# A two-layer encoder trunk: the recurrent scan without its engine loop, and squares for a norm taken in the gate before it

## The chip, the cores and the metric

The kernel runs on one core of a Trainium2 chip. The metric is the device time of one execution in microseconds (us), the median over runs. The engines are TensorE (PE in the rows), VectorE (DVE), ScalarE (ACT), GpSimd (POOL) and SyncE (SP); PEld is TensorE's weight load.

## The reference, cut to what matters

Two layers run over 1024 prompt and 64 sample positions of 1024 features. Layer 0 mixes tokens with a gated convolution and attention; layer 1 is a recurrent layer (RWKV-7). Each layer then has a channel mixer and a gated embedding:

```python
def rms_norm(x, g):
    y = x32 * lax.rsqrt(jnp.mean(x32 * x32, axis=-1, keepdims=True) + NORM_EPS)
    return (y * g.astype(jnp.float32)).astype(x.dtype)
...
        hn = rms_norm(h, W['mix_norm_pre'][i])
...
        gate = jax.nn.sigmoid(rms_norm(h, W['ple_norm'][i]) @ W['ple_gate'][i])
        h = h + gate * (p[i].astype(h.dtype) @ W['ple_proj'][i])
```

The recurrent mixer carries a state through time, per head of 64 (16 heads):

```python
    def step(S, inp):
        r_t, w_t, k_t, v_t, kk_t, b_t = inp
        sa = jnp.einsum('bhvk,bhk->bhv', S, -kk_t)
        S = S * w_t[:, :, None, :] + sa[..., None] * b_t[:, :, None, :] + v_t[..., None] * k_t[:, :, None, :]
        return S, jnp.einsum('bhvk,bhk->bhv', S, r_t)
```

## The kernel before, in words

All activations are feature-major: `H`, `A`, `B`, `TM` are SBUF tiles of 128 partitions by some 8, 8, 22 and 4 blocks of T = 1092 columns (both groups of positions with padding), `ps` is PSUM. Each engine has a hand-written program; they meet at semaphores. A class `Tally` counts what each semaphore will have reached. Inside `t.loop(n, ...)` a stretch is emitted once and repeated by the engine itself (`Fori`, L111, which sets a register, computes wait values from it and branches back), with the growth of each count per turn as arguments.

**The gated embedding** (`channel_mixer`, end). For each of the 8 blocks of features PE makes the gate's product (72 matmuls, L466) and the projection of `p` (6 matmuls, L440), ACT takes the sigmoid (L1270), DVE multiplies (L1848) and adds into `H` (L1851), and then splits the next weights into an upper and a lower part (L1578, L1579). DVE does it in `ple_tiles`: a loop of 3 turns of two blocks, and two blocks after it.

**The norm ahead of layer 1.** When the last block of `H` is there, ACT squares the 8 blocks one by one (L1071, called from the program's line L1284) into two alternating buffers of `TM`, and PE sums each over the features with a matrix of ones (`norm_direct`, L498, three matmuls per block, accumulated in PSUM). The two alternate, since a buffer is free again only when PE has read it. Then ACT takes the logarithm and the exponential (`root`, L1078 and L1081), and DVE scales the 8 blocks (`pre_norm`, L1537).

**The scan of layer 1** goes over 16 chunks of 64 prompt positions, then one of the sample. One chunk is one call of `chunk` on PE, ACT, DVE and POOL. Each pipelines three chunks: the state of chunk c (`from_state` L926 and L929, `solve` L937, `outputs` L952 and L955, `to_state` L962), the inverse of a triangular matrix for chunk c + 1 by five levels (`y` L903 on PE, copied by ACT L1424; `z` L912 on PE, taken by DVE L2040 and turned L2029), and the products of chunk c + 2 (`gram` L863, masked by DVE L2060 and L2066; `turn_n` L878). POOL loads chunk c + 3 and sets up a matrix (L2354). In each engine chunks 0 to 11 are a loop of three turns with four chunks in its body (PE's is at L1026 to L1029), and chunks 12 to 15 are written out behind it.

In the body of a loop a wait's value depends on the turn, so the queue computes it in a register ahead of the wait (L851 in `await_`); in written-out chunks it is a constant.

Of the kernel before, what the change touches and what calls it, by code (L numbers as in the profile page):

```python
# [24 lines left out]
ALU = mybir.AluOpType  # L25
# [5 lines left out]
KT = D // P  # L31
SEQ, DEC, PAST = 1024, 64, 2048
PAD = 2
P0 = PAD
S0 = PAD + SEQ + PAD
T = S0 + DEC
NCH = 3
CH = T // NCH
# [8 lines left out]
NP_ = PLE // P  # L47
HR = 16
NPAIR = HR // 2
C = 64  # L50
NCHUNK = SEQ // C
# [33 lines left out]
NL = len(LEVELS) - 1  # L85
# [54 lines left out]
def build_trunk(nc, I, O, stop=99):  # L140
    ctx = ExitStack()
    with ctx:
# [15 lines left out]
        H = sb("H", [P, KT, T])  # L158
# [70 lines left out]
        CV = [kv[:, PAST:2 * PAST].rearrange("p (b n) -> p b n", b=16) for kv in KV]  # L229
        Vt = Bf[:, 16 * T:16 * T + 9 * 512].rearrange("p (b n) -> p b n", b=9)  # L230
        HEAD = [slice(0, C), slice(C, P)]


        Lb = [{n: B[:, 4 * u + j, :] for j, n in enumerate("rkwa")} for u in range(2)]
# [53 lines left out]
        def k(name):  # L288
            o, n = CST[name]
            return cst[:, o:o + n]  # L290
# [7 lines left out]
        def pset(s):  # L298
# [12 lines left out]
        d_v = scratch("d_v", [NPAIR, P, (NCHUNK + 1) * C])  # L311


        names = ["setup", "held", "x_in", "mm_done", "read0", "read1", "w_used", "wl_ready", "xh_ready", "xl_ready", "h_out", "h_in", "sq_ready", "sq_used", "rs_ready",
                 "normed", "h_ready", "act_step", "dve_step", "pool_step", "out_done",
                 "wv_in", "wv_ready", "tm_free", "ax_ready", "p_in",
                 "cum_ready", "cum_out", "cum_in", "lf_e", "logf_out", "ckt_done", "ckt_ready", "mb_done", "mb_read", "x_add", "x_ready", "v_done", "r_log", "r_ready", "qn_ready", "cumk_in", "kv_in2", "kv_in3", "turn_done", "s_done", "s_read", "e_ready",
# [102 lines left out]
        def _(pe):  # L420
            t = Tally(pe)
# [332 lines left out]
                return  # L754


            norm_direct()
            t.up("normed", KT)
            X = [[B[:, 8 * b + j, :] for j in range(KT)] for b in range(2)]

# [262 lines left out]
                    gram(1, 1)  # L1023
                z(l, 1)
            turn_n(1, 0)
            with t.loop(3, z_dup=4, g_done=8, g_ready=8, tok_read=16, n_done=8, m_first=8, m_ready=8 * NL, n_ready=8, mt_ready=8 * NL,  # L1026
                        y_ready=8 * NL, c_in=8, a_ready=8, u_ready=8, oo_read=8):
                for c in range(4):
                    chunk(c)  # L1029
            for c in range(12, NCHUNK):  # L1030
                chunk(c, prepare=c + 2 <= NCHUNK)
            for g in range(2):
                await_("m_ready")
# [29 lines left out]
        def _(act):  # L1063
            t = Tally(act)

            def square(src, needs=None):

                j = t.n.get("sq_ready", 0) % 2
                if t.some("sq_ready", -1):
                    act.wait_ge(S["sq_used"], t.val("sq_ready", -1))  # L1070
                nc.scalar.activation(TM[:, j, :], src, ACT.Square).then_inc(S["sq_ready"], 1)  # L1071
                t.up("sq_ready")
# [206 lines left out]


            log_and_exp()
            act.wait_ge(S["h_ready"], t.val("h_ready"))
            for j in range(KT):
                square(H[:, j, :])  # L1284
            root()
            act.wait_ge(S["dve_p"], t.up("dve_p"))

# [197 lines left out]
                for g in range(2):  # L1485
                    take_y(g)
            turned_n(1, 0)
            with t.loop(3, y_done=8 * NL, n_done=8, tok_done=8, a_done=8, u_done=8, oo_done=8) as i:
                for c in range(4):
                    chunk(c, i * (4 * C) + (P0 + C * c))  # L1490
            for c in range(12, NCHUNK):
                chunk(c, P0 + C * c, prepare=c + 2 <= NCHUNK)
            for g in range(2):
                from_state(g)
# [33 lines left out]
        def _(dve):  # L1528
# [30 lines left out]
                dve.wait_ge(S["rs_ready"], t.up("rs_ready"))  # L1559

            def pre_norm(gain):
                t.up("sq_ready", KT)
                t.up("sq_used", KT)
                rstd()
                for j in range(KT):
                    stt(A[:, j, :], H[:, j, :], v1(gain, j), TM[:, 3, :], ALU.mult, ALU.mult).then_inc(S["normed"], 1)
                    t.up("normed")
# [212 lines left out]
            def channel_mixer(l):  # L1780
# [58 lines left out]
                def ple_tiles(i, last):  # L1839
                    for j in range(2):  # L1840
                        if not (last and j == 1):
                            split_chunk()
                            t.skip_chunks(1)
                        s, mm, rd = t.unit()
                        dve.wait_ge(S[f"read{s}"], rd)
                        s, mm, rd = t.unit()
                        dve.wait_ge(S["mm_done"], mm)
                        nc.vector.tensor_tensor(c3(TM[:, j, :]), pset(s), c3(TM[:, j, :]), ALU.mult).then_inc(S[f"read{s}"], 1)  # L1848
                        dve.wait_ge(S[f"read{s}"], rd)
                        h = H[:, KT - 2 + j, :] if last else H[:, bass.ds(i * 2 + j, 1), :].rearrange("p a n -> p (a n)")  # L1850
                        nc.vector.tensor_tensor(h, h, TM[:, j, :], ALU.add).then_inc(S["h_ready"], 1)  # L1851
                        t.up("h_ready")

                with t.loop(KT // 2 - 1, mm_done=4, read0=2, read1=2, h_ready=2, chunk=4, w0=16, w1=16, w2=16, w3=16,
                            wl_ready=2, wh=2, dve_step=2) as i:
                    ple_tiles(i, False)
                ple_tiles(None, True)

# [254 lines left out]
            for l in range(NL):  # L2113
# [7 lines left out]
                    masked(1, 1, 0)  # L2121
                    masked(1, 1, 1)
                take_z(0, l, 1)
            with t.loop(3, g_done=8, m_init=4, m_first=8, m_ready=8 * NL, z_done=8 * NL, st_done=8, st_read=8) as i:
                for c in range(4):
                    chunk(c, bass.ds(i * 4 + c, 1))
            for c in range(12, NCHUNK):
                chunk(c, slice(c, c + 1), prepare=c + 2 <= NCHUNK)
            for g in range(2):
                new_state(slice(NCHUNK, NCHUNK + 1), g)  # L2130
# [31 lines left out]
        def _(pool):  # L2162
# [214 lines left out]
            double_chunk(2)  # L2377
            pool.wait_ge(S["hs_out"], 16)
            pool.dma_start(H[:, :, :], d_h).then_inc(S["hs_in"], 16)
            with t.loop(3, u_done=8, tok_done=8, zi0=96, zi1=96) as i:  # L2380
                for c in range(4):
                    chunk(c, i * 4 + c)
            for c in range(12, NCHUNK):
                chunk(c, c, prepare=c + 2 <= NCHUNK, load=c + 3 <= NCHUNK)
            pool.wait_ge(S["c_in"], 2 + 2 * NCHUNK)
            store(O["wkv"][:, 0], ST)
# [148 lines left out]
```

## Time and profile before

| | us |
|---|---|
| median of 3 runs | 4018.39 |
| lowest, highest | 4010.32, 4018.71 |
| the profiled execution, its own time | 4018.97 |
| span of its trace | 4017.2 |
| mean granted clock of TensorE | 0.951 of full |

The page says for each engine how long it was busy (PE 91% of the span, DVE 38%, ACT 21%, POOL 5%), and in its part 4 which chain of work ended last. A wait is named by what released it; "issue" is time in which an engine waited for nothing that the profile shows. PEclk is the granted clock: 1.00 is 2.4 GHz, 0.50 is 1.2 GHz. The names of PEldq and the like are the queues that feed the engines.

### The profile page before, as it was taken

Reading aid. Unit: us, or ns where it says so; the run is one execution under the profiler, and the core shown is the slowest. Engines: PE = TensorE matmul, PEld = TensorE weight load, DVE = VectorE, ACT = ScalarE, POOL = GpSimd, SP = SyncE. Lnnn points to the kernel's source line nnn. Section 1 sums busy time; section 2 is a strip of 40 time slices with the busy share of each in tenths; the row PEclk is TensorE's granted clock in tenths of the full one; section 3 lists DMA queues with packets and bytes.
Section 4 is the critical chain, followed back from the end, with each engine's and each line's share of the span. In section 5 each row is a group of like instructions: output and inputs, shape, how many; then the busy total and the mean of one; then the engine's idle time right before and its main releaser. Section 6 shows DMA issues by size and latency. Waiting matters only on the chain.

```text
span 4017.2 us, 66019 instructions
## 1 busy us (share of the span) xinstructions
PE 3646.6 (91%) x28466; PEld 3290.3 (82%) x28466; DVE 1540.8 (38%) x2029; ACT 856.4 (21%) x1134; POOL 207.1 (5%) x347
## 2 busy tenths in 40 slices
PE   6999999899999999889988688888698999999977
PEld 4997337799999999666987577787488999999967
DVE  3143554432212222536338644444734221222352
ACT  2000332210000010228225323233422000001020
POOL 0000000000000000001002211110100000000000
PEclk8999998899999999899998799889999999999989
DMA  2122002111121130124226621111411112113111
GB/s 89 60 77 80 22 22 82 71 43 47 42 82 53 42 129 29 49 75 171 87 104 254 237 86 52 46 42 34 147 60 54 42 39 80 60 44 120 42 39 69
DMA packets 79399, 301.59 MB, mean 75 GB/s; under 512 B 13560, under 2 KB 15880, under 8 KB 75192
## 3 DMA queue, kind: packets, MB, share of 16 engines
q0 software_dynamic: 36816, 174.51, 11.9%
q1 hardware_dynamic: 42368, 123.92, 9.9%
q8 instruction: 172, 2.82, 0.3%
q14 instruction: 43, 0.35, 0.0%
HBM read 217.29 MB, written 81.10 MB: 74 GB/s over the span
## 4 chain that ended last, share of the span: by engine, by line
PE 73%; DVE 7%; issue 2%; ACT 2%; DMA 1%; POOL 0%; DVEq 0%; ACTq 0%; POOLq 0%
PE ps L466 55%; DVE A L1537 2%; PE ps L912 2%; PE ps L903 2%; PE ps L480 2%; PE ps L440 1%; PE ps L773 1%; PE ps L863 1%; DVE H L1618 1%; DVE A_r L1594 1%; PE ps L498 1%; PE ps L926 1%; PE ps L929 1%; PE ps L878 1%; DVE B L1537 1%
## 5 line engine op out<-in xcount | busy, mean ns | idle before, releaser
L466 PE MATMUL ps<-H_r,W_r 128*128 128x364 f32 (+1 forms) x3192 | 705.8, 329 | 0.0
L466 PE MATMUL ps<-H_r,TM_r 128*128 128x364 f32 x2736 | 607.5, 330 | 21.6 <-DVE A_r L1594 18.0
L466 PE MATMUL ps<-A_r,TM_r 128*128 128x364 f32 x2736 | 606.2, 330 | 0.0
L466 PEld LDWEIGHTS ps<-H_r,W_r 128*128 128x128 f32 (+1 forms) x3192 | 556.3, 188 | 1.8
L466 PEld LDWEIGHTS ps<-H_r,TM_r 128*128 128x128 f32 x2736 | 475.9, 189 | 28.0 <-issue 19.8
L466 PEld LDWEIGHTS ps<-A_r,TM_r 128*128 128x128 f32 x2736 | 476.9, 189 | 0.0
L466 PE MATMUL ps<-B_r,DW_r 128*128 128x364 f32 x2112 | 408.8, 329 | 0.0
L466 PE MATMUL ps<-B_r,W_r 128*128 128x364 f32 x1824 | 404.8, 330 | 0.0
L466 PEld LDWEIGHTS ps<-B_r,DW_r 128*128 128x128 f32 x2112 | 358.8, 188 | 0.0
L466 PEld LDWEIGHTS ps<-B_r,W_r 128*128 128x128 f32 x1824 | 319.7, 190 | 0.0
L1800 DVE TENSOR_TENSOR TM<-ps,TM 128x1092 f32<-128x1092 f32 x44 | 57.0, 1296 | 444.1 <-PE ps L466 444.1
L466 PE MATMUL ps<-B_r 128*128 128x364 f32 x960 | 195.6, 334 | 13.9 <-DVE B_r L1605 13.9
L1578 DVE CAST TM_r<-W 128x1024 fp32r<-128x1024 f32 x114 | 78.7, 690 | 312.0 <-PE ps L466 301.9
L466 PE MATMUL ps<-B_r,TM_r 128*128 128x364 f32 x768 | 177.0, 339 | 17.1 <-DVE A_r L1594 17.1
L466 PEld LDWEIGHTS ps<-B_r 128*128 128x128 f32 x960 | 168.3, 193 | 15.1 <-issue 15.1
L1235 ACT ACTIVATE B_r<-TM 128x1092 f32 (+1 forms) x44 | 49.2, 1118 | 542.7 <-DVEq L1802 542.7
L498 PE MATMUL ps<-TM,cst 128*128 128x364 f32 x288 | 107.8, 532 | 55.2 <-ACT TM L1071 55.2
L466 PEld LDWEIGHTS ps<-B_r,TM_r 128*128 128x128 f32 x768 | 135.7, 192 | 23.7 <-issue 13.8
L2040 DVE COPY_PREDICATED B<-lvl,ps 128x256 f32<-128x256 uint8 x170 | 75.2, 443 | 187.2 <-PE ps L912 186.5
L498 PEld LDWEIGHTS ps<-TM,cst 128*128 128x128 f32 x288 | 60.2, 216 | 104.3 <-issue 65.6
L903 PE MATMUL ps<-B 64*64 64x64 f32 x2720 | 120.6, 229 | 25.5 <-issue 10.8
L1578 DVE CAST DW_r<-W 128x768 fp32r<-128x768 f32 x64 | 33.6, 525 | 282.9 <-PE ps L466 282.9
(303 smaller groups left out, 4444.5 us busy)
## 6 DMA issues: line engine op xcount, KB each, us to landing
W<-in_wgu SPq DMA_DIRECT2D x88, 512.0 KB, 3.6
H<-d_h POOLq DMA_DIRECT2D x3, 4368.0 KB, 23.1
W<-in_wdown SPq DMA_DIRECT2D x32, 384.0 KB, 3.1
W<-in_wrkv SPq DMA_DIRECT2D x24, 512.0 KB, 3.6
W<-in_wdown SPq DMA_DIRECT2D x32, 320.0 KB, 2.9
d_h<-H POOLq DMA_DIRECT2D x16, 546.0 KB, 3.0
d_y<-TM POOLq DMA_DIRECT2D x16, 546.0 KB, 3.4
A<-d_y POOLq DMA_DIRECT2D x16, 546.0 KB, 8.0
```

Source lines behind the costliest of these rows:

```text
L440: ins = nc.tensor.matmul(ps[0:cols, NCH * s + c, 0:CH], W[0:rows, slot, j * cols:(j + 1) * cols], xs[n][0:rows, c * CH:(c + 1) * CH], star ...
L466: ins = nc.tensor.matmul(ps[0:cols, NCH * s + c, 0:CH], w[:, j * cols:(j + 1) * cols], x[k1][:, c * CH:(c + 1) * CH], start=(k1 == 0 and n ...
L480: ins = nc.tensor.matmul(ps[:, NCH * s + c, 0:CH], lhs, x[:, c * CH:(c + 1) * CH], start=True, stop=True)
L498: ins = nc.tensor.matmul(ps[:, NCH * s + c, 0:CH], k("ones"), TM[:, j % 2, c * CH:(c + 1) * CH], start=(j == 0), stop=(j == KT - 1))
L773: ins = nc.tensor.matmul(ps[:, NCH * s + c, 0:CH], W[:, slot, j * P:(j + 1) * P], X[b][j][:, c * CH:(c + 1) * CH], start=(j == 0), stop=(j ...
L903: ins = nc.tensor.matmul(ps[r, g, C * a:C * a + C], AB[c % 2][r, p, :], Ms[c % 2][r, p, :], start=True, stop=True)
L912: ins = nc.tensor.matmul(ps[r, g, 256 + C * a:256 + C * a + C], MT[r, p, :], Y[r, p, :], start=True, stop=True)
L1235: nc.scalar.activation(hi, TM[:, j, :], ACT.Copy).then_inc(S["mid_hi"], 1)
L1537: return nc.vector.scalar_tensor_tensor(out=out, in0=in0, scalar=scalar, in1=in1, op0=op0, op1=op1)
L1578: step(nc.vector.tensor_copy(wh, w))
L1800: nc.vector.tensor_tensor(c3(TM[:, j, :]), pset(s), c3(TM[:, j, :]), ALU.mult).then_inc(S[f"read{s}"], 1)
L2040: nc.vector.copy_predicated(Ms[c % 2][:, 4 * g:4 * g + 4, :], four(lvl[:, l + 1, :]), half_of(g, 256)).then_inc(S["m_ready"], 1)
```

## The change

Two edits. The first: in all four engines the loop of the scan is dropped and `chunk` is called for c = 0 to 15 in a plain Python loop, so that all 16 chunks are written out. The second: in layer 0's embedding gate DVE, after it has added a block into `H`, squares that block into a free block of `B` (`HSQ`) and adds the square into another (`HSUM`); of the last block it leaves the square in `HSQ`. PE makes the sum over features from these two alone, 3 + 3 matmuls accumulated; ACT squares nothing there. The diff shows PE's two places, then ACT's norm, then DVE's gate; the scan loops of ACT (L1488), DVE (L2124) and POOL (L2380) are dropped as PE's is.

```diff
+        HSUM, HSQ = B[:, NP_ + KT, :], B[:, NP_ + KT + 1, :]
...
-            norm_direct()
+            s, mm, rd = t.unit()
+            pe.wait_ge(S[f"read{s}"], t.val(f"read{s}", -1))
+            for n, x in enumerate((HSUM, HSQ)):
+                pe.wait_ge(S["h_sums"], n + 1)
+                for c in range(NCH):
+                    ins = nc.tensor.matmul(ps[:, NCH * s + c, 0:CH], k("ones"), x[:, c * CH:(c + 1) * CH],
+                                           start=(n == 0), stop=(n == 1))
+            ins.then_inc(S["mm_done"], 1)
             t.up("normed", KT)
...
             turn_n(1, 0)
-            with t.loop(3, z_dup=4, g_done=8, g_ready=8, tok_read=16, n_done=8, m_first=8, m_ready=8 * NL, n_ready=8, mt_ready=8 * NL,
-                        y_ready=8 * NL, c_in=8, a_ready=8, u_ready=8, oo_read=8):
-                for c in range(4):
-                    chunk(c)
-            for c in range(12, NCHUNK):
+            for c in range(NCHUNK):
                 chunk(c, prepare=c + 2 <= NCHUNK)
...
             log_and_exp()
-            act.wait_ge(S["h_ready"], t.val("h_ready"))
-            for j in range(KT):
-                square(H[:, j, :])
             root()
...
                         nc.vector.tensor_tensor(h, h, TM[:, j, :], ALU.add).then_inc(S["h_ready"], 1)
                         t.up("h_ready")
-
+                        if l:
+                            continue
+                        dve.wait_ge(S["h_ready"], t.val("h_ready"))
+                        if last and j == 1:
+                            nc.vector.tensor_tensor(HSQ, h, h, ALU.mult).then_inc(S["h_sums"], 1)
+                        else:
+                            step(nc.vector.tensor_tensor(HSQ, h, h, ALU.mult))
+                            step(nc.vector.tensor_tensor(HSUM, HSUM, HSQ, ALU.add))
+                        if last and j == 0:
+                            dve.sem_inc(S["h_sums"], 1)
+
+                if l == 0:
+                    step(nc.vector.memset(HSUM, 0.0))
                 with t.loop(KT // 2 - 1, mm_done=4, read0=2, read1=2, h_ready=2, chunk=4, w0=16, w1=16, w2=16, w3=16,
-                            wl_ready=2, wh=2, dve_step=2) as i:
+                            wl_ready=2, wh=2, dve_step=2 if l else 6) as i:
                     ple_tiles(i, False)
                 ple_tiles(None, True)
```

How the instructions move, in the two places of the argument. The change is one line longer at the top and eight more further down, so its lines are numbered otherwise.

PE, the last matmuls of the loop's body and the turn of the loop, before (L912 is `z`, L863 `gram`, L878 `turn_n`, L903 `y`):

```order
L912 MATMUL ps<-TM 64x64 x8
L860 REGISTER_ALU
L863 MATMUL ps<-B 128x128 x8
L851 REGISTER_ALU
L912 MATMUL ps<-TM 64x64 x8
L878 MATMUL ps<-cst,B 64x64 x8
L111 REGISTER_ALU
L111 COMPARE_AND_BRANCH
L903 MATMUL ps<-B 64x64 x8
```

The same place in the change, between chunk 3 and chunk 4 (L920, L871, L886, L911 are the same four):

```order
L920 MATMUL ps<-TM 64x64 x8
L871 MATMUL ps<-B 128x128 x8
L920 MATMUL ps<-TM 64x64 x8
L886 MATMUL ps<-cst,B 64x64 x8
L911 MATMUL ps<-B 64x64 x8
```

The matmuls stand in the same order; the branch and the register operations ahead of waits are gone.

DVE, one block of the embedding loop, before (the multiply, the add into `H`, the split of weights):

```order
L1848 TENSOR_TENSOR TM<-ps,TM 128x1092
L1849 REGISTER_ALU
L1851 ISA
L1851 TENSOR_TENSOR H<-H,TM 128x1092
L1576 REGISTER_ALU
L1578 CAST TM_r<-W 128x1024
L1534 REGISTER_ALU
L1579 TENSOR_TENSOR W_r<-W,TM_r 128x1024
```

and in the change:

```order
L1844 TENSOR_TENSOR TM<-ps,TM 128x1092
L1845 REGISTER_ALU
L1847 ISA
L1847 TENSOR_TENSOR H<-H,TM 128x1092
L1851 REGISTER_ALU
L1855 TENSOR_TENSOR B<-H 128x1092
L1532 REGISTER_ALU
L1856 TENSOR_TENSOR B<-B 128x1092
L1532 REGISTER_ALU
L1572 REGISTER_ALU
L1574 CAST TM_r<-W 128x1024
L1532 REGISTER_ALU
```

The square and its sum stand ahead of the split of the next weights.

## Rows read from the trace of the kernel before

**Rows 1.** The page: its head, and the shares of the chain of waits, part 4

```profile
span 4017.2 us, 66019 instructions
...
PE 73%; DVE 7%; issue 2%; ACT 2%; DMA 1%; POOL 0%; DVEq 0%; ACTq 0%; POOLq 0%
```

**Rows 2.** Chain of waits, 1765 to 1806 us: start us, us, what

```profile
1765.99 3.69 PE ps L440 x12
...
1771.10 1.31 DVE H L1851
...
1772.43 1.12 ACT TM L1071
...
1773.69 16.62 PE ps L498 x48
...
1790.34 1.18 ACT TM L1078
...
1791.54 1.12 ACT TM L1081
...
1792.68 10.23 DVE A L1537 x8
```

**Rows 3.** Chain of waits, whole span: the six-matmul sum of a norm, twice

```profile
2128.23 1.85 PE ps L480 x6
...
3827.84 4.02 PE ps L480 x6
```

**Rows 4.** Timeline of DVE, first embedding gate: start, us, instruction [idle before <-releaser]

```profile
1660.23 1.30 DVE L1848 TENSOR_TENSOR TM<-ps,TM 128x1092 f32<-128x1092 f32 x1 [3.88 <-PE ps L440]
...
1675.86 1.29 DVE L1848 TENSOR_TENSOR TM<-ps,TM 128x1092 f32<-128x1092 f32 x1 [11.02 <-PE ps L440]
1677.33 1.30 DVE L1851 TENSOR_TENSOR H<-H,TM 128x1092 f32 x1 [0.17 <-DVE TM L1848]
1678.54 0.69 DVE L1578 CAST TM_r<-W 128x1024 fp32r<-128x1024 f32 x1
1679.26 1.22 DVE L1579 TENSOR_TENSOR W_r<-W,TM_r 128x1024 fp32r<-128x1024 f32 x1
```

**Rows 5.** Windows, one scan step each: us, busy (count) by engine, PEclk, DMA share

```profile
2357.10:2384.50 27.40, 23.60 (x614) 21.18 (x612) 14.16 (x32) 9.64 (x25) 4.53 (x6) 1.00 0.19 51
2384.50:2412.60 28.10, 23.52 (x616) 21.10 (x614) 14.18 (x32) 9.75 (x25) 4.44 (x7) 1.00 0.19 50
...
2440.10:2471.35 31.25, 24.69 (x615) 22.87 (x612) 14.38 (x32) 9.67 (x25) 4.40 (x7) 0.89 0.18 46
...
2557.60:2589.70 32.10, 25.65 (x614) 23.44 (x612) 14.38 (x32) 9.66 (x25) 4.42 (x6) 0.89 0.18 45
...
2619.60:2649.50 29.90, 26.39 (x614) 24.16 (x612) 14.18 (x32) 9.65 (x25) 4.41 (x6) 0.83 0.18 47
2649.50:2678.00 28.50, 24.82 (x614) 23.06 (x612) 14.18 (x32) 9.68 (x25) 4.41 (x6) 0.88 0.18 49
...
2707.80:2736.00 28.20, 25.08 (x616) 23.27 (x614) 14.21 (x32) 9.78 (x25) 4.46 (x7) 0.88 0.19 49
2736.00:2765.30 29.30, 26.11 (x612) 24.09 (x610) 14.20 (x32) 9.62 (x25) 4.38 (x6) 0.83 0.18 48
```

**Rows 6.** Timeline of PE at two turns of the loop and in two steps without

```profile
2400.91 0.94 PE L863 MATMUL ps<-B 64*128 64x128 f32 x13 [1.41 <-issue]
...
2461.21 1.12 PE L903 MATMUL ps<-B 64*64 64x64 f32 x16 [3.65 <-issue]
...
2580.35 1.12 PE L903 MATMUL ps<-B 64*64 64x64 f32 x16 [3.39 <-issue]
...
2726.57 1.12 PE L903 MATMUL ps<-B 64*64 64x64 f32 x16 [0.73 <-ACT B L1428]
```

**Rows 7.** Line L111, the loops' own instructions: duration ns min/median/max

```profile
L111 PEldq COMPARE_BRANCH  x49: 67/207/3582, 149.9 to 3991.2; - x49
```

**Rows 8.** Line L851, one step's register operations on PE's queue

```profile
L851 PEldq ALU_OP  x12: 32/32/32, 2415.2 to 2439.9; - x12
```

More of the change, by code:

```diff
@@ L311, in build_trunk @@
         d_v = scratch("d_v", [NPAIR, P, (NCHUNK + 1) * C])
-        names = ["setup", "held", "x_in", "mm_done", "read0", "read1", "w_used", "wl_ready", "xh_ready", "xl_ready", "h_out", "h_in", "sq_ready", "sq_used", "rs_ready",
+        names = ["setup", "held", "x_in", "mm_done", "read0", "read1", "w_used", "wl_ready", "xh_ready", "xl_ready", "h_out", "h_in", "sq_ready", "sq_used", "rs_ready", "h_sums",
                  "normed", "h_ready", "act_step", "dve_step", "pool_step", "out_done",
@@ L1487, in _ @@
             turned_n(1, 0)
[L1488 to L1491, printed above, removed]
+            for c in range(NCHUNK):
                 chunk(c, P0 + C * c, prepare=c + 2 <= NCHUNK)
@@ L1561, in pre_norm @@
             def pre_norm(gain):
-                t.up("sq_ready", KT)
-                t.up("sq_used", KT)
                 rstd()
@@ L2123, in _ @@
                 take_z(0, l, 1)
[L2124 to L2127, printed above, removed]
+            for c in range(NCHUNK):
                 chunk(c, slice(c, c + 1), prepare=c + 2 <= NCHUNK)
@@ L2379, in _ @@
             pool.dma_start(H[:, :, :], d_h).then_inc(S["hs_in"], 16)
[L2380 to L2383, printed above, removed]
+            for c in range(NCHUNK):
                 chunk(c, c, prepare=c + 2 <= NCHUNK, load=c + 3 <= NCHUNK)
```

## The prediction

> **What bounds the kernel now.** I read the page first. TensorE holds 73% of the chain that ended last [rows 1], and most of that is dense matmul that this change leaves as it is. So the change can pay only where PE waits. Then the chain of waits in order of time, around the two places of the diff.
>
> At the end of layer 0 the last projection ends at 1769.68 us, the last block of `H` at 1772.41, and DVE begins to scale for layer 1 at 1792.68 [rows 2]. Between them stand one square on ACT, 16.62 us of `norm_direct` on PE (eight small sums, each waiting for the next square), the logarithm and the exponential. Nothing else of the program moves: these 20.25 us (1772.43 to 1792.68) are exposed in full.
>
> In the scan the windows, cut where POOL sets up its matrix, give the length of a step [rows 5]. Fourteen steps go from 2357.1 to 2765.3: 408.2 us, 29.2 each. The reader is to see three kinds: 27.4 and 28.1 us with the granted clock at 1.00; 28.5 and 29.9 with it at 0.88 and 0.83; 31.25 and 32.1 where the loop turns. The last two rows are written-out steps, and they are 28.2 and 29.3: being written out makes no step short by itself. The timeline of PE shows what a turn is: PE stands idle for 3.65 and 3.39 us ahead of the first `y` of the body, "issue" being named, where a written-out step waits 0.73 for ACT [rows 6]. The branch itself shows it: PE's branches take 207 ns in the median but up to 3582 ns [rows 7].
>
> **Edit 1, the norm.** Removed: the eight squares on ACT and 24 matmuls. Added on the path: one square on DVE over the same 128x1092, about 1.30 as the add of that shape [rows 4], 0.14 to reach PE (1773.55 to 1773.69 in [rows 2]), then three matmuls of `HSQ`. The three of `HSUM` go behind the last projection, which ends 2.7 us before the last block of `H`. The rows show a sum as six records (three fp32 matmuls): 1.85 us at the high clock, 4.02 at the low one [rows 3]. PE has been busy just before, but there is a gap of 2 us; I take 2.9 between the two. Logarithm and exponential stay: 1790.31 to 1792.68 is 2.37. Sum: 1.30 + 0.14 + 2.9 + 2.37 = 6.7 against 20.25, a gain of **13.5 us**, with 14.6 and 12.4 as the ends by the two clocks.
>
> Beside other work: in the loop DVE does 2 x 1.30 more per block ahead of the split of weights (0.69 + 1.22). It idles 11.02 us per block waiting for the projection [rows 4], so a block has room for 2.6. The cover would be gone only if this exceeded 11. The memset of `HSUM` has no row; between 0 and 1.30 us (an add of its shape reads two operands more), once, ahead of the loop where DVE then idles 3.88 us [rows 4]: nothing. ACT loses eight squares that nobody else waited for. What is late next is DVE's scaling of 8 blocks, 10.23 us, unchanged.
>
> **Edit 2, the scan.** It has four terms.
>
> - The two turns back: (3.65 - 0.73) + (3.39 - 0.73) = 5.6 us. The exit of the loop has no such stall, since its branch is not taken. The loops' ends on ACT, DVE and POOL go as well; PE waits for none of them there, so I count nothing, and up to 1 us a turn as a gain the range can hold.
> - Register operations: 12 of 32 ns in a step for `await_` alone [rows 8], some 0.4 us on PE's own queue. Compared at the same clock, loop against written out: 28.5 to 28.2 at 0.88, and 29.9 to 29.3 at 0.83 [rows 5]. I take 0.4 a step, twelve steps: 4.8 us.
> - The clock. PEclk falls in a step when PE has paused at its end; a step with it at 0.83 or 0.88 costs 1.1 to 2.5 us more than one at 1.00 (27.4). Both turns of the loop are pauses of the longest kind and have low clock in their step. Whether steps without them hold the clock can't be read off: the first two did, the written-out two did not.
> - A stall inside `gram`: PE stops for 1.41 us amid sixteen matmuls of one group, no semaphore between them [rows 6]. I take it for the wait for the next instructions, since nothing else is left. The change shifts where in a step such waits fall, either way.
>
> Bounds for the last two together come from steps: all fourteen like the two written-out ones, 28.75, make 402.5, a gain of 5.7 (with all four terms in it). All at full clock, 27.4 less 0.4 = 27.0, make 378, a gain of 30. I take the middle, 27.9 a step, 390.6, a gain of **17.6 us**: 10.4 from turns and register operations, 7 from a clock that holds in half of the steps that lose it now.
>
> The Trainium skill (Runtime: NRT & Kernel Launch, Instruction fetch mechanics) says that instructions are prefetched in sequence, that a taken branch out of the window stalls, and that otherwise the fetch is hidden. On the branch the trace agrees, with 3.65 us; on the rest it does not, with 1.41 us in the middle of a group. Were it hidden in written-out code, the result would be near the 27.0 of the upper bound.
>
> **Sum.** 4018.97 (the profiled execution, 0.6 above the median of 4018.39) - 13.5 - 17.6 = 3987.9, say **3988**. A difference of 0.2%, 8 us, is about what a measurement of this kernel can tell from none.
>
> **The rivals.**
> - *The clock keeps falling.* Every step is like the two written-out ones: 4018.97 - 13.5 - 5.7 = 3999.8. For it: the only written-out steps with a successor. Against: two steps of the loop with the same matmuls hold 1.00, and the low clock of the later ones comes after a turn.
> - *The clock holds throughout* and no arrival of instructions shows: 4018.97 - 13.5 - 30 = 3975.5. For it: 27.4 us at 2357, in a step with all register operations. Against: low clock in the written-out steps, some 10 us and more behind the last turn.
> - *The branch is nearly free.* The stall of 3.65 us is then the arrival of the next instructions, which straight code has too, and only the register operations go: 4018.97 - 13.5 - 4.8 = 4000.7. For it: the 1.41 us; the median of 207 ns. Against: no written-out step shows an idle of that size. The Trainium skill (Advanced Engine Details and Errata, Control Flow Timing) has about 108 ns for compare-and-branch, which speaks for this rival; the longest here is 3582 ns.
> - *Slower.* Sixteen chunks of straight code have to be brought in on four queues, and arrivals like that of 1.41 us come more often and on DVE and ACT too, each pause lowering the clock. It decides once a step exceeds (408.2 + 13.5) / 14 = 30.1 us. With three more such stalls on 28.75 a step is 33.0, so 462 us: 4018.97 - 13.5 + 53.5 = 4059. Against: the two written-out steps on the same four queues, 28.2 and 29.3.
> - *The change does not do what it says in the norm*: the squares come late, since DVE is behind on weights. That needs DVE to lose its 11.02 us of idle time; then the norm gives nothing and the scan's gain stays, 4001.4.
>
> **How the numbers follow.** Forecast 0.52. Clock keeps falling 0.20, clock holds 0.14, branch nearly free 0.06, norm without gain 0.02, slower 0.04; 0.02 for a gain within 8 us. The number is the likeliest one. The range takes in the first three cases with 1.1 us for the price of the sums and a few us around the scan: 3972 to 4003. Faster by over 0.2%: 0.94; within 0.2%: 0.02; slower: 0.04.
>
> **What would show it.** In the profile after: DVE begins to scale 6 to 8 us after the last block of `H`, not 20; PE idles nowhere in the scan for over 3 us; no register operations stand on the queues there; the step is 27 to 28.7 us, at 1.00 where it is 27. It is wrong in the norm if the gates' period, 15.66 us from 1660.23 to 1675.86 less 0.03, grows; in the scan if windows without a turn are over 29 us, or if a pause of 3 us stands in straight code.

## The result, and the profile after

The changed kernel takes **3958.01 us** (median of 4 runs, 3955.37 to 3959.47) against 4016.52 for the kernel before (4 runs, 4010.32 to 4018.71): a ratio of 0.9854 [0.9837, 0.9871], 58.5 us less. The forecast was 3988 with a range of 3972 to 4003: the sign was right, the forecast gain (31 us) was half of what came, and the time lies below the range.

The page of the kernel after, its head, the shares of its chain of waits and the queue that brings instructions (packets, MB, share):

```profile
span 3956.3 us, 65294 instructions
...
PE 73%; DVE 7%; ACT 2%; issue 2%; DMA 1%; POOL 0%; DVEq 0%; ACTq 0%; POOLq 0%
...
q8 instruction: 168, 2.75, 0.3%
```

The span is 60.9 us shorter than before, with the shares of the chain as they were [rows 1]. Where it went, by the same events in both traces:

| stretch | before | after | difference |
|---|---|---|---|
| start to the end of the last block of `H` | 1772.41 | 1770.83 | -1.6 |
| from there to DVE's scaling for layer 1 | 20.25 | 7.32 | -12.9 |
| preparation of layer 1, up to the scan's first products | 513.7 | 512.0 | -1.7 |
| those to the first step | 50.8 | 54.0 | +3.2 |
| fourteen steps of the scan | 408.2 | 362.4 | -45.8 |
| the rest | 1251.9 | 1249.8 | -2.1 |

**The norm.** The chain of waits after, at the end of layer 0 (start, duration, what):

```profile
1769.52 1.31 DVE H L1847
...
1770.85 1.31 DVE B L1853
...
1772.20 3.60 PE ps L763 x6
...
1775.83 1.18 ACT TM L1082
...
1777.03 1.12 ACT TM L1085
...
1778.17 10.23 DVE A L1535 x8
```

The square, six records of matmul, the logarithm and the exponential stand where 16.62 us of `norm_direct` stood [rows 2]. In the loop the two additional operations of DVE lie beside PE's work. The timeline of DVE in an embedding block after:

```profile
1677.08 1.30 DVE L1855 TENSOR_TENSOR B<-H 128x1092 f32 x1
1678.41 1.30 DVE L1856 TENSOR_TENSOR B<-B 128x1092 f32<-128x1092 f32 x1
...
1689.94 1.30 DVE L1844 TENSOR_TENSOR TM<-ps,TM 128x1092 f32<-128x1092 f32 x1 [7.78 <-PE ps L441]
```

DVE's idle time per block fell from 11.02 us [rows 4] to 7.78, and the period of a block stayed at 15.66.

**The scan.** Windows after (from:to, length, busy time of PE, PEld, DVE, ACT and POOL, granted clock, DMA share, GB/s). The first five are single steps, the last is all fourteen:

```profile
2344.10:2369.30 25.20, 22.89 (x615) 20.94 (x612) 14.22 (x32) 9.82 (x25) 4.44 (x7) 1.00 0.21 55
2369.30:2394.70 25.40, 22.75 (x614) 20.82 (x612) 14.23 (x32) 9.81 (x25) 4.41 (x7) 1.00 0.21 55
2419.40:2444.20 24.80, 22.42 (x614) 20.59 (x612) 14.22 (x32) 9.71 (x25) 4.42 (x7) 1.00 0.22 56
2545.70:2572.50 26.80, 23.13 (x616) 20.94 (x613) 14.29 (x32) 9.74 (x25) 4.42 (x7) 1.00 0.19 52
2652.00:2680.30 28.30, 23.96 (x616) 22.03 (x612) 14.30 (x32) 9.71 (x25) 4.42 (x7) 0.94 0.18 49
2344.10:2706.50 362.40, 320.37 (x8519) 294.09 (x8516) 199.55 (x448) 136.41 (x337) 61.80 (x85) 0.98 0.20 54
```

Here is the surprise: the same 612 or so matmuls take 24.8 to 25.4 us in good steps. No step of the kernel before is under 27.4, not even at full clock with no turn in it [rows 5]. That is neither the turn nor the clock. The later steps of the changed kernel get slower again (26.8, 28.3), though nothing in the code tells one step from another. What PE waits for in the fourteen steps after (us in total, times, longest):

```profile
PE ps L911 <- issue: 12.9, 9, 3.3
PE ps L871 <- DVE B L2074: 11.9, 9, 1.4
PE ps L911 <- ACT B L1429: 10.2, 14, 0.7
```

And the timeline of PE inside the step of 28.3 us:

```profile
2667.03 0.47 PE L911 MATMUL ps<-B 64*64 64x64 f32 x3 [3.34 <-issue]
2667.31 1.12 PE L920 MATMUL ps<-TM 64*64 64x64 f32 x16
```

A pause of 3.34 us stands in straight code, among the `y` of one step, with no branch near. The forecast named just this as a sign that it is wrong.

### The profile page after: what moved, and what is told of

Its sections match the earlier page's. It is cut to its first block, busy times and chain, and to the rows that moved or that the text cites. A ratio compares the mean times of both kernels' runs of the same rounds, so it can differ in the third digit from the quotient of the medians.

```text
span 3956.3 us, 65294 instructions
## 1 busy us (share of the span) xinstructions
PE 3603.4 (91%) x28430; PEld 3254.8 (82%) x28430; DVE 1562.7 (40%) x2045; ACT 848.0 (21%) x1126; POOL 206.7 (5%) x347
## 3 DMA queue, kind: packets, MB, share of 16 engines
q8 instruction: 168, 2.75, 0.3%
## 4 chain that ended last, share of the span: by engine, by line
PE 73%; DVE 7%; ACT 2%; issue 2%; DMA 1%; POOL 0%; DVEq 0%; ACTq 0%; POOLq 0%
PE ps L467 56%; DVE A L1535 2%; PE ps L920 2%; PE ps L911 2%; PE ps L441 1%; PE ps L481 1%; PE ps L781 1%; DVE H L1614 1%; PE ps L871 1%; DVE A_r L1590 1%; DVE B L1535 1%; PE ps L898 1%; PE ps L960 1%; PE ps L934 1%; PE ps L937 1%
## 5 line engine op out<-in xcount | busy, mean ns | idle before, releaser
L467 PEld LDWEIGHTS ps<-H_r,TM_r 128*128 128x128 f32 x2736 | 475.5, 189 | 28.2 <-issue 19.8
L467 PEld LDWEIGHTS ps<-B_r,TM_r 128*128 128x128 f32 x768 | 135.1, 191 | 24.8 <-issue 13.8
L911 PE MATMUL ps<-B 64*64 64x64 f32 x2720 | 115.3, 222 | 29.3 <-issue 13.3
L1575 DVE TENSOR_TENSOR W_r<-W,TM_r 128x1024 fp32r<-128x1024 f32 x114 | 139.7, 1225 | 3.9
L499 PE MATMUL ps<-TM,cst 128*128 128x364 f32 x240 | 92.5, 543 | 50.8 <-ACT TM L1075 50.7
## 6 DMA issues: line engine op xcount, KB each, us to landing
W<-in_wgu SPq DMA_DIRECT2D x88, 512.0 KB, 3.2
W<-in_wrkv SPq DMA_DIRECT2D x24, 512.0 KB, 3.3
```

The costliest lines, as they stand in the source:

```text
L467: ins = nc.tensor.matmul(ps[0:cols, NCH * s + c, 0:CH], w[:, j * cols:(j + 1) * cols], x[k1][:, c * CH:(c + 1) * CH], start=(k1 == 0 and n ...
L499: ins = nc.tensor.matmul(ps[:, NCH * s + c, 0:CH], k("ones"), TM[:, j % 2, c * CH:(c + 1) * CH], start=(j == 0), stop=(j == KT - 1))
L911: ins = nc.tensor.matmul(ps[r, g, C * a:C * a + C], AB[c % 2][r, p, :], Ms[c % 2][r, p, :], start=True, stop=True)
L1575: nc.vector.tensor_tensor(Wr[:, slot, 0:n], w, wh, ALU.subtract).then_inc(S["wl_ready"], 1)
```

## The theory: where PE's blocks of instructions end

Three theories were set against each other. **Loop**: the gain is that of the turns and register operations, in the main. **Clock**: it is that of a clock that no longer falls. **Place**: PE's instructions arrive in blocks, PE pauses where a block is late, and the change moved the blocks' ends to another place in each step.

For Place speaks the queue of instruction fetches (q8): 2.75 MB in 168 packets, 16.4 KB each. The Trainium skill (Runtime: NRT & Kernel Launch, Instruction fetch mechanics) gives such a block as 16 KiB or 256 instructions. The trace agrees: 168 blocks of 256 are 43,008 instructions, and PE's changed program has 43,257. I counted the instructions of PE's program. A written-out step has 1271, nine under five blocks (1280), so from step to step a block's end moves nine instructions deeper into the step. A step of the loop has 1286, and the end moves back by six. As a measure I take the **offset**: how many instructions behind the start of the step's last `gram` the next block ends. Its origin was set once, by the pauses in the traces of before and after; the experiments are what tests it. The offsets are 13, 7, 1 and -5 in the loop's body before, and 1, 10, 19 behind it. After, they run from 108 to 234 by nines.

The offset is moved by idle instructions: an increment of a semaphore that nobody waits for (`held`). Placed ahead of the scan they move all steps alike ("fill"; the last of them is merged with the wait behind it, so the program grows by one less than the diff says). Inside the step they change how the offset drifts ("pad"). In the diffs, `chunk` is PE's.

## The experiments

Each was timed in one batch with the kernel before on the same chip: 4017.24 us for the first four, 4014.21 for the next four, 4019.49 for the last four. So times of different batches can be compared to some 5 us, and ratios are safer. All rows "fourteen steps" are read as above, from one profiled execution of each kernel.

**1. The norm's edit alone; the loops stay.**

```diff
+                        if last and j == 1:
+                            nc.vector.tensor_tensor(HSQ, h, h, ALU.mult).then_inc(S["h_sums"], 1)
+                        else:
+                            step(nc.vector.tensor_tensor(HSQ, h, h, ALU.mult))
+                            step(nc.vector.tensor_tensor(HSUM, HSUM, HSQ, ALU.add))
...
-            norm_direct()
+            for n, x in enumerate((HSUM, HSQ)):
+                pe.wait_ge(S["h_sums"], n + 1)
...
```

> The edit of the norm alone; the scan's loop stands in all engines. Two theories for the 45.8 us that fourteen scan steps lost in the change. Loop: the loop's own instructions (branch, register operations) cost them; then this kernel gains the norm's 12.9 us and nothing in the scan, some 4003 to 4004, with scan steps of 27.4 to 32 as before. Place: what counts is where in a step PE's instruction stream reaches the end of a block of instructions that has to be fetched; the norm's edit makes PE's stream 73 instructions shorter ahead of the scan, so the ends move from 13 to -5 instructions behind the start of the step's last gram (turns of four steps: 13, 7, 1, -5) to 86, 80, 74, 68 behind it; then the scan gets faster too, though nothing of it was edited: 15 to 30 us more, 3974 to 3989.

Measured: 3971.68 us, ratio 0.9883 [0.9861, 0.9905], fourteen steps:

```profile
2337.10:2717.90 380.80, 324.69 (x8520) 295.58 (x8518) 199.11 (x448) 136.88 (x337) 62.20 (x85) 0.99 0.20 52
```

An edit that does not touch the scan shortens it by 27 us, to steps of 25.3 to 27.2 (30.7 where it turns) with the clock at 0.99 in place of 0.90. Loop can't do that. The edit takes 73 instructions from PE's stream, so the offsets move from 13...-5 to 86...68. The time is 2 us under what Place expected.

**2. The same, with the 73 instructions given back.**

```diff
+            for _ in range(73):
+                pe.sem_inc(S["held"], 1)
             pe.wait_ge(S["st_ready"], 1)
```

> As the kernel with the norm's edit alone, and 73 semaphore increments put in on PE ahead of the scan, where PE waits for the first chunk anyway. They put the ends of the blocks back where they were in the kernel before (14, 8, 2, -4). Loop and Place both expect the norm's gain alone here: 4003 to 4005, 12 to 13 us under before. If it is as fast as the one without the 73, Place is wrong.

Measured: 3998.61 us, ratio 0.9955 [0.994, 0.997].

```profile
2334.50:2738.90 404.40, 346.26 (x8518) 315.83 (x8516) 199.43 (x448) 135.66 (x337) 62.19 (x85) 0.92 0.19 49
```

73 instructions that do nothing cost 27 us, and the scan is back at 404.4 (408.2 before). The kernel is some 5 us faster than expected, 3.8 of them in the scan.

**3. The kernel before with 128 idle instructions ahead of the scan, nothing else.** The same edit with `range(128)`; offsets 142 to 124.

> The kernel before with nothing edited but 128 semaphore increments on PE ahead of the scan, in time in which PE waits. Loop expects no change or up to some 5 us slower, 4016 to 4021. Place expects a faster kernel from idle instructions: the ends of the blocks lie 142, 136, 130, 124 instructions behind the last gram, as in the change's quick steps; 15 to 30 us faster, 3986 to 4002.

Measured: 3972.33 us, ratio 0.9874 [0.9846, 0.9901]. A step, one with a turn, and all fourteen:

```profile
2358.70:2384.10 25.40, 22.61 (x616) 20.74 (x614) 14.13 (x32) 9.83 (x25) 4.47 (x7) 1.00 0.20 55
2434.80:2466.30 31.50, 24.56 (x615) 22.70 (x613) 14.27 (x32) 9.71 (x25) 4.42 (x7) 0.89 0.18 46
2358.70:2721.70 363.00, 318.73 (x8520) 293.34 (x8518) 198.58 (x448) 136.56 (x337) 61.82 (x85) 0.98 0.21 54
```

The old kernel's scan, loops and all, falls by 45.2 us, as much as the change's. The time is 14 us under the expected 3986 to 4002: the sign of Place was expected, its size was not. Two things follow. Place is the larger cause. And a turn can be priced for the first time: 31.5 and 31.1 us beside steps of 24.5 to 25.7, some 6 us each.

**4. The scan's edit alone; the norm stays.** Offsets 35 to 161, from the bad place into the good one within one run.

```diff
-            with t.loop(3, z_dup=4, g_done=8, ...):
...
+            for c in range(NCHUNK):
                 chunk(c, prepare=c + 2 <= NCHUNK)
```

> The scan written out in all four engines, the norm as before. Loop expects the change's time plus the norm's 12.9 us: 3971. Place expects that too or less, since the 73 instructions put the ends of the blocks at 35 to 161 behind the last gram in place of 108 to 234, and the change's slow steps (26.2 to 28.3 us, from the ninth on) had 180 to 234: the late steps should fall to some 25.3 us, 12 us less, 3958 to 3965; the early steps, at 35 to 98, are at places that no run has shown yet.

Measured: 3965.45 us, ratio 0.9874 [0.9845, 0.9902]. All fourteen, the third, and 25 us late in the scan:

```profile
2346.00:2714.60 368.60, 320.99 (x8518) 292.98 (x8516) 199.75 (x448) 136.71 (x337) 62.69 (x85) 1.00 0.20 53
2401.20:2431.90 30.70, 24.75 (x617) 22.32 (x612) 15.17 (x34) 9.84 (x25) 4.61 (x6) 0.94 0.17 46
2600.00:2625.00 25.00, 22.41 (x602) 20.47 (x600) 13.95 (x32) 9.81 (x24) 4.41 (x6) 1.00 0.23 58
```

In order the steps are 28.2, 27.8, 30.7, 27.3, 27.6, 26.2, 25.5, 25.7, 25.2, 24.9, 25.0, 24.5, 25.2, 24.9: slow at offsets of 35 to 80, quick from some 90 on. The first two have the granted clock at 1.00, as the quick ones have, so a falling clock (Clock) is not what makes them slow. The kernel after shows the other border: 24.7 to 25.9 up to an offset of some 170, 25.3 to 28.3 behind it.

**5. The change with five idle instructions in each step**, ahead of the last `gram`. They slow the drift to four per step: offsets 103 to 159, all in the good place.

```diff
                 if prepare:
+                    for _ in range(5):
+                        pe.sem_inc(S["held"], 1)
                     gram(c + 2, 1)
```

> The changed kernel with five semaphore increments on PE in each step, ahead of the last gram, where PE waits for DVE some 1.4 us anyway. A step is then 1276 instructions in place of 1271, and the end of a block of 256 wanders by 4 per step, not 9: it lies 103 to 159 instructions behind the last gram in all steps, where the quick steps of three kernels had it (24.5 to 25.4 us). Place expects fourteen steps of 25.0, 350 us in place of 362.4: 3946 us, from 85 instructions more. A theory that sees only work and waits expects the change's 3958, or up to 3 us more.

Measured: **3941.02 us** (5 runs, 3938.42 to 3951.22), ratio 0.9823 [0.9804, 0.9842]: the lowest time of the study, with 75 instructions more than the change. It is 17 us less by the medians and 12 by the two ratios; 11.3 of them stand in the scan.

```profile
2337.40:2688.50 351.10, 315.35 (x8520) 289.72 (x8518) 198.93 (x448) 137.00 (x337) 61.84 (x85) 1.00 0.21 56
```

The waits of PE in these steps:

```profile
PE ps L871 <- DVE B L2076: 18.8, 14, 1.4
PE ps L911 <- ACT B L1431: 10.3, 14, 0.9
PE ps L911 <- issue: 2.7, 5, 1.3
```

The pauses put down to "issue" shrank from 12.9 us to 2.7 at L911. Instead `gram` now waits in every step for DVE's masks, which comes last and was there in nine steps of the change.

**6. The change, locked in the bad place.** Nine idle instructions per step make a step exactly five blocks; 94 ahead of the scan set the offset to 6 in all steps. Code as in 5 with `range(9)`, and as in 2 with `range(94)`.

> The changed kernel with nine semaphore increments per step at the same spot and 94 ahead of the scan. A step is 1280 instructions, five blocks, so the end of a block stays 6 instructions behind the start of the last gram in every step, the place of the kernel before. Place expects steps of 28 to 30 us in code without any loop: 392 to 420 us for fourteen, 3988 to 4016 in all, nearly the whole gain of the scan lost again. If it stays near 3958, the loop was the cause after all.

Measured: 3993.22 us, ratio 0.9955 [0.9941, 0.9968], every step 27.3 to 29.2.

```profile
2341.90:2739.60 397.70, 341.57 (x8520) 312.06 (x8518) 198.85 (x448) 136.12 (x337) 61.95 (x85) 0.93 0.19 49
```

This is the change with the place of before. Against before's 408.2 it leaves 10.5 us to the loops and register operations together.

**7. Only PE written out; ACT, DVE and POOL keep their loops.** PE's stream is that of the change.

The edit, against the change, on ACT (on DVE and POOL alike):

```diff
-            for c in range(NCHUNK):
+            with t.loop(3, y_done=8 * NL, n_done=8, tok_done=8, a_done=8, u_done=8, oo_done=8) as i:
+                for c in range(4):
+                    chunk(c, i * (4 * C) + (P0 + C * c))
+            for c in range(12, NCHUNK):
```

> The change with the scan written out on PE alone; ACT, DVE and POOL keep their loops. PE's stream, and with it the place of its blocks, is the change's to the instruction. If the other engines' branches and register operations are covered, it takes the change's 3958 within 3 us; if they lie on the path, up to 10 us more.

Measured: 3963.63 us, ratio 0.9879 [0.9856, 0.9902]. All fourteen, and the first step with a turn of the three:

```profile
2339.40:2708.50 369.10, 323.04 (x8520) 295.77 (x8518) 198.95 (x448) 136.28 (x337) 61.80 (x85) 0.98 0.20 53
2414.60:2443.50 28.90, 24.02 (x612) 22.01 (x611) 14.24 (x32) 9.76 (x25) 4.41 (x6) 0.94 0.19 49
```

The scan is 6.7 us over the change's. The two turning steps alone are 8.6 us longer (28.9 and 29.3 where the change has 24.8 and 24.8), the twelve others 2 us shorter. In the turning steps PE waits for DVE (L2040), 2.0 us at most. The difference of the whole kernels, 5.6 us, is within the intervals of the two ratios; it is the two steps that show it.

**8. The reverse: PE keeps its loop, the others are written out.** PE's offsets are those of 1.

> The counterpart: PE keeps its loop, the other three are written out, the norm is the new one. PE's stream is that of the kernel with the norm's edit alone (3971.7 us, steps that turn 30.7 us each). Expected: the same 3972 within 3 us, with both turning steps at 30 to 31 us. If the turning steps shrink to some 28, the other engines' turns were part of their price.

Measured: 3972.4 us, ratio 0.9903 [0.9881, 0.9924].

```profile
2336.10:2715.90 379.80, 325.45 (x8518) 296.61 (x8515) 199.02 (x448) 137.17 (x337) 62.04 (x84) 0.99 0.20 52
```

As in 1, 380.8: with PE turning as well, the turns of the others cost nothing that can be seen. They lie beside PE's.

**9. Norm edited, loops kept, in the good place.** Experiment 1 with 201 idle instructions ahead of the scan; offsets 142 to 124.

> The new norm, the loop in all four engines, and 201 semaphore increments on PE ahead of the scan, which put the ends of the blocks at the good place (142, 136, 130, 124 behind the last gram). It prices the loop with the place held: against the kernel with five increments per step (3941.0 us, written out, 103 to 159) it has two turns and the register operations more. Expected 3959: the kernel before with 128 increments (3972.3) less the norm's 12.9 us. The scan's fourteen steps some 363 us, two of them at 31.

Measured: 3966.89 us, ratio 0.9866 [0.9849, 0.9884].

```profile
2348.40:2714.50 366.10, 320.06 (x8518) 294.67 (x8516) 198.67 (x448) 136.34 (x337) 61.80 (x84) 0.98 0.21 54
```

The scan came as placed, with turns of 31.0 and 31.9. The whole was 8 us slower than I had expected, since the 201 instructions are themselves partly exposed: from the sum of the norm to the scan's first products 523.3 us pass, against 518.0 in experiment 5. The other 3 us are the scan's (366.1 against the expected 363).

**10. The old norm, all written out, in the good place.** Experiment 4 with five per step and 183 ahead; offsets 104 to 160.

> The counterpart of the kernel with five increments per step, with the old norm: scan written out, five increments per step, 183 ahead of the scan, so that the ends lie at 104 to 160 as there. It prices the norm with the place held: 12.9 us above 3941.0, so 3954. If the chain's 12.9 us were partly given back later, it would be less than 3954.

Measured: 3960.41 us, ratio 0.9852 [0.9837, 0.9867]. The scan, and the old norm in its chain:

```profile
2356.00:2709.60 353.60, 316.07 (x8520) 290.03 (x8518) 199.00 (x448) 137.26 (x337) 61.96 (x85) 1.00 0.21 55
```

```profile
1766.54 16.62 PE ps L498 x48
```

It stands 19.4 us above experiment 5, where the norm alone should make 13, but only 12 by the two ratios, since the kernel before was 5 us slower in this batch. The profiles show, beside the norm, 2.6 us of exposed fill (PE waits 29.4 us ahead of the scan's first products, 26.8 in experiment 5) and 2.5 us of the scan. So the whole times can't confirm the norm's size. The chains can: from the last block of `H` to DVE's scaling, the four kernels with the old norm have 20.3 us each, the ten with the new one 6.9 to 7.4.

**11 and 12. A step of exactly five blocks, with the offset locked at 217 and at 131.** Nine per step, and 139 or 225 ahead; the two differ in 86 idle instructions.

```diff
-            for _ in range(139):
+            for _ in range(225):
                 pe.sem_inc(S["held"], 1)
```

> The change with nine increments per step and 139 ahead of the scan: the end of a block stays 217 instructions behind the last gram (39 ahead of the next end's gram) in every step, the place of the change's slowest step (28.3 us). Place expects steps of 27 to 28.5, 378 to 399 us for fourteen, 3974 to 3995 in all.

> The same with 225 ahead of the scan: the end stays at 131 in every step. Place expects steps of 24.6 to 25.0 us, 344 to 350 for fourteen, 3935 to 3941 in all, so as fast as or a little faster than the kernel with five increments (3941.0). 86 idle instructions more than the kernel with 139, and some 40 us less, if Place is right.

Measured: **4011.88 us** at 217, ratio 0.9983 [0.9971, 0.9995]; **3947.11 us** at 131, ratio 0.9819 [0.9804, 0.9834]. At 217, a step and all fourteen, then PE's waits:

```profile
2397.60:2427.90 30.30, 26.27 (x614) 24.18 (x612) 14.29 (x32) 9.72 (x25) 4.43 (x6) 0.83 0.18 47
2339.10:2759.00 419.90, 357.70 (x8518) 329.99 (x8514) 200.19 (x448) 135.99 (x337) 61.93 (x84) 0.85 0.18 47
```

```profile
PE ps L920 <- issue: 40.4, 14, 3.5
PE ps L871 <- issue: 11.3, 14, 0.9
PE ps L911 <- ACT B L1433: 10.2, 14, 0.7
```

At 131 all fourteen steps, then PE's waits:

```profile
2346.00:2696.50 350.50, 315.09 (x8519) 289.98 (x8516) 198.92 (x448) 137.49 (x337) 61.98 (x85) 1.00 0.21 56
```

```profile
PE ps L871 <- DVE B L2078: 19.8, 14, 1.4
PE ps L911 <- ACT B L1433: 10.3, 14, 0.8
PE ps L911 <- issue: 2.9, 8, 0.5
```

At 217 PE pauses in every step for up to 3.5 us at L920 and then 0.8 at L871: 51.7 us in all. None of the program's semaphores is named, and the wait for DVE's masks is gone, since the pause covers it. At 131 the masks' wait and the pauses come to 22.7 us, so that is 29 us more; the rest of the 69.4 us between the two scans goes with the clock, 0.85 against 1.00, at which PE's busy time is 42.6 us longer. This was worse than I had expected of 217 (3974 to 3995): in the kernel after, the steps at 207 to 225 took 26.2 to 28.3 us. The case is Place's worst, and it nearly cancels the whole change. At 131 the scan is as short as anywhere. The 225 instructions are exposed by some 9 us (527.0 against 518.0), which put the kernel 6 us above what was expected; by ratio it can't be told from experiment 5 (0.9819 and 0.9823).

**What the traces show of the late blocks.** Each trace has the time at which every block came in on q8. In all fourteen scans PE's matmuls start more than 2 us apart in 46 places. In every one of them a block lands meanwhile, and PE goes on 1.2 to 2.2 us after it has landed. That is the pause as a wait for instructions, seen in the trace.

What is under way while a block is late stands there too: POOL's load of chunk c + 3 (`d_bk`, `d_ar`, `d_v`). In each step it moves its data for some 6 us. In experiment 11, from 2374.5 to 2379.2 us, ahead of such a block, the queues show (packets, MB, share):

```profile
q0 software_dynamic: 313, 1.16, 93.2%
```

and the pause behind it:

```profile
2382.04 0.98 PE L920 MATMUL ps<-TM 64*64 64x64 f32 x15 [2.97 <-issue]
```

The blocks before and behind this stretch begin at 2371.80 and 2379.32, 7.5 us apart, where about five fit into an undisturbed step of 25 us. In experiment 12 one begins at 2378.02, 0.7 us ahead of the load's data, and the next at 2384.05. It is so in all kernels: in the 196 steps of the fourteen scans, only 12 blocks begin between 0.5 and 4 us behind the start of the load's data, and 166 between 4.5 and 5.5 us. It looks as if a block that falls due in the load has to come behind it, and as if the good place were the one in which a block still begins just ahead of the load. The load in its turn waits for PE (in the kernel before, its rows name L890, `token_major`, as what released it), which ties it to a place in PE's step. This is read from the traces of all fourteen kernels; no run moved the load or took it away, so that it is the load that holds the block up is likely, not shown.

## Why the prediction was half right

**The norm: right.** 13.5 us forecast, 12.9 measured, from the same pieces: square 1.31 (1.30), three matmuls 3.60 (2.9), logarithm and exponential 2.3 (2.37). The price of the sum was near the low-clock end that I had kept. The cover held: DVE still idles 7.78 us per block.

**Turns and register operations: right in sum, wrong in their parts.** I forecast 5.6 + 4.8 = 10.4 us. With the place held nearly alike, loop against written out gives 408.2 - 397.7 = 10.5 (before, experiment 6), 363.0 - 353.6 = 9.4 (experiments 3 and 10) and 366.1 - 351.1 = 15.0 (9 and 5). But the turns carry nearly all of it: 6 us each in the good place, not the 2.8 that I took from PE's idle time. In experiment 3 two pauses stand behind the first turn, and only the first is the one that I had counted:

```profile
2454.68 0.68 PE L903 MATMUL ps<-B 64*64 64x64 f32 x16 [3.94 <-issue]
...
2457.08 0.90 PE L878 MATMUL ps<-cst,B 64*64 64x64 f32 x10 [1.48 <-issue]
```

The rest goes with the clock, 0.89 in this step: PE is busy for 24.56 us in it, against 22.61 in the quick one. The register operations are not to be seen: the twelve steps without a turn of experiment 3 mean (363.0 - 31.5 - 31.1) / 12 = 25.03 us, and those of experiment 5, which has none of them but five idle instructions, 25.1. That ACT, DVE and POOL turn costs nothing as long as PE turns too (experiment 8), and 6.7 us once PE does not (7). "PE waits for none of them" held for the kernel before, not for a kernel half changed.

**The step that failed is the last one of the sum, "bounds for the last two together come from steps".** I took 27.4 us less 0.4 = 27.0 as the floor of a step, because it was the best row of before at full clock, and 7 us for a clock that holds. All steps of before, the written-out ones too, lay at offsets from -5 to 19: the rows agreed with each other since they shared one bad place, and none of them showed a good one. The floor is 24.5 to 25.5. The fourteen steps of the change mean 25.9 us (362.4 / 14), under the 27.9 that I took and under the floor too. The term of 7 us measured 45.8 - 10.5 = 35 us; with the others near their forecast, that is 28 of the 30 us by which the forecast missed. What the term left out is the move of PE's block ends out of their bad place. I had the mechanism in hand: the gram stall of 1.41 us [rows 6] was read rightly as a wait for instructions (a block lands at 2399.50, PE goes on at 2400.91), and I wrote that the change shifts where such waits fall, "either way". Then I priced it from steps that the shift had not touched. The clock was a follower: it is low in steps with the long pauses (0.83 with those of up to 3.5 us in experiment 11, 1.00 where they are gone).

**The rivals.** "The clock holds throughout" (3975.5) is nearest, but for its reason, that no arrival of instructions shows, the traces say otherwise: they show in the change too, 12.9 us at L911. "Branch nearly free" falls by experiment 3. The rows of the branches themselves in the kernel before, at the first turn, and PE's instruction queue in the 3 us from 2457 on:

```profile
L111 PEldq COMPARE_BRANCH  x1: 3550/3550/3550, 2456.9 to 2456.9; - x1
...
L111 DVEq COMPARE_BRANCH  x1: 67/67/67, 2457.3 to 2457.3; - x1
```

```profile
q8 instruction: 1, 0.02, 2.1%
```

PE's branch takes 3.55 us, and one block is fetched for it meanwhile. DVE's takes 67 ns by its record, but the next instruction of DVE's queue stands at 2460.5, some 3 us later: a short record does not mean a short turn. "Slower" asked for pauses like 1.41 us in straight code, each lowering the clock, and for 30.1 us a step. As a mechanism this rival is real: experiment 11 has 30.0 us a step, and 4011.88. Whether the change shows it or its opposite was decided by where 256-instruction blocks happened to end. I gave it 0.04 and no term in the range; a count of PE's instructions in both programs could have told that the offset moves by 95, though not to which side the time would go.

The Trainium skill (Runtime: NRT & Kernel Launch, Instruction fetch mechanics) has a taken branch out of the window stall, and the traces agree with 3.55 us. It also has the fetch hidden otherwise, and the crossing of a block's end mostly hidden. For this scan the runs show the contrary: 350.5 against 419.9 us with the same matmuls.

**How much of the 58.5 us is the change's own?** About 13 for the norm and 9 to 15 for the loops. The remaining 30 to 36 are the place: 73 instructions less by the norm and 22 less by the scan's edit ahead of the first step (offset 13 to 108), and a step that is shorter by 15. Experiment 3 gets 45 from the old kernel without either edit.

**Left open.** Whether POOL's load is what makes the arrival late at offsets near 0 and 217 and not at 131: the traces point to it, but the load was not moved. The wait for DVE's masks does not tell the places apart, for it is there in every step at the bad offset 6 and at the good 131 alike (19.8 us in fourteen steps, both). Nor was it tried to move the ends of blocks on ACT, DVE and POOL. Up to 12 us between two profiles lie ahead of some 814 us, in code that no edit touches, and are not explained.

## What to carry to other kernels

Where one engine's code is dense and runs to thousands of instructions, count them: an edit that adds or drops instructions also moves every later block end on that engine, and in this kernel that was worth up to 65 us, more than the edit. Before crediting an edit, repeat it with idle instructions that restore the old position, and try two or three positions of the kernel before as well; a repeating stretch can be held in its best place by padding it to, or near, a multiple of 256 (experiments 5 and 12). Look in the profile at when the blocks come in, and at which loads are under way then. And a floor taken from the best row of before is a floor only for what the rows of before share.

## What the runs showed of the hardware that I had not expected

- PE, in straight code with no branch, pauses for up to 3.5 us per step for instructions, and whether it does depends on the block's end: 86 more idle instructions ahead of the scan made 4011.88 into 3947.11 us.
- Instruction blocks hardly ever begin to come in during the first 4 us of a load's data (12 in 196 steps); 166 begin 4.5 to 5.5 us behind its start.
- A taken branch of PE costs 6 us in all where the surroundings are good (31.5 against 25.0 us): pauses of 3.94 and 1.48 us, the rest with the clock at 0.89 in the step.
- Turns of three other engines cost 6.7 us together with PE written out, and 1.0 us (380.8 against 379.8), which is nothing clear of noise, with PE looping.
- Idle semaphore increments are not free where PE has nothing else to do: 201 and 225 of them cost 5 and 9 us ahead of the scan, while 139 cost nothing there. Five per step inside the scan cost nothing that can be seen.
